# The `steps` stage of a hybrid layer taken into its samples' attention, and attention's rows stored tile by tile

## The reference

```
mod = silu(c) @ w_ada + b_ada            # 9 rows of c: the prompt's and 8 samples'
sh1, sc1, g1, sh2, sc2, g2 = split(mod, 6)
h = rmsnorm(x) * (1 + sc1) + sh1
z, xs, bm, cm, dtr, q, k, v, qi, ki, wi, gs, ga = split(h @ w_in)
# prompt: the indexer picks 256 keys per query, then softmax attention over them
# samples: the same over 256 cached keys in pages of 128 (a page table) and the new key
dt = softplus(dtr + dt_bias); A = -exp(a_log)
Acs = cumsum(dt * A) in chunks of 128    # decays of the chunked scan (32 heads)
xbc = silu(conv(xs, bm, cm))             # depthwise, causal, width 4
y_ssm = scan(xbc, dt, A) * silu(z), normed
x = x + g1 * ((sig(gs) * (y_ssm @ w1) + sig(ga) * (y_attn @ w2)) @ w_out)
h2 = rmsnorm(x) * (1 + sc2) + sh2
x = x + g2 * swiglu(h2)
```

## Time and profile before

| | |
|---|---|
| median of three runs | 2975.42 us |
| profiled execution, whole run | 2976.01 us |
| its span | 2974.3 us |
| busy in the span: PE, DVE, POOL, ACT | 2755.2, 1540.4, 810.6, 680.6 us |
| samples' attention | 942.8 to 1026.3 us of the span |
| `steps` | 1026.3 to 1087.2 us |
| start of `stream` | 1087.2 us |

### The profile page before, as it was taken

The page is one execution under the profiler, slowest core; times in us unless marked ns, Lnnn a source line. Parts: engine busy times, 40 slices in busy tenths (PEclk is TensorE's granted clock), DMA queues, the critical chain, the costliest instruction groups (busy, mean ns, idle before and its releaser), DMA issues. The chain is left out here.

```text
span 2974.3 us, 40645 instructions
## 1 busy us (share of the span) xinstructions
PE 2755.2 (93%) x16375; PEld 2343.0 (79%) x16375; DVE 1540.4 (52%) x2733; ACT 680.6 (23%) x1432; POOL 810.6 (27%) x486
## 2 busy tenths in 40 slices
PE   7999999998996678999979979998889999999997
PEld 4888556666785468999966669998878989898986
DVE  3313399905553357666459953554634242525155
ACT  3121211105774211221247731101210000000001
POOL 0000530004321124434326642231232222232220
PEclk9999999997998679999989989999989999999999
DMA  6110234520002144334156644333111111111111
GB/s 220 50 54 22 68 121 151 170 74 9 2 2 100 56 127 149 130 120 140 57 146 198 183 148 131 113 100 108 29 44 52 49 43 43 43 44 46 54 29 57
DMA packets 288663, 258.63 MB, mean 87 GB/s; under 512 B 21273, under 2 KB 265361, under 8 KB 288290
## 3 DMA queue, kind: packets, MB, share of 16 engines
q1 hardware_dynamic: 254780, 190.35, 21.3%
q10 hardware_dynamic: 26176, 56.16, 5.2%
q0 software_dynamic: 7520, 9.51, 1.0%
HBM read 191.04 MB, written 65.06 MB: 86 GB/s over the span
## 5 line engine op out<-in xcount | busy, mean ns | idle before, releaser
L2283 PE MATMUL ps<-h_lo,w_hi 128*128 128x344 f32 x1504 | 483.2, 321 | 18.0 <-DVE h_lo L2402 11.2
L2284 PE MATMUL ps<-h_hi,w_hi 128*128 128x344 f32 x1504 | 482.0, 321 | 0.0
L2285 PE MATMUL ps<-h_hi,w_lo 128*128 128x344 f32 x1504 | 481.9, 320 | 0.0
L2265 POOL CAST w_hi<-ring 128x2048 fp32r<-128x2048 f32 (+1 forms) x50 | 96.9, 1938 | 812.8 <-PE ps L2285 784.8
L2283 PEld LDWEIGHTS ps<-h_lo,w_hi 128*128 128x128 f32 x1504 | 284.5, 189 | 19.1 <-issue 18.4
L2285 PEld LDWEIGHTS ps<-h_hi,w_lo 128*128 128x128 f32 x1504 | 284.5, 189 | 0.0
L2284 PEld LDWEIGHTS ps<-h_hi,w_hi 128*128 128x128 f32 x1504 | 284.2, 189 | 0.2
L2283 PE MATMUL ps<-s_h_lo,s_w_hi 128*128 128x344 f32 x816 | 266.0, 326 | 0.0
L2284 PE MATMUL ps<-s_h_hi,s_w_hi 128*128 128x344 f32 x816 | 261.1, 320 | 0.0
L2285 PE MATMUL ps<-s_h_hi,s_w_lo 128*128 128x344 f32 x816 | 261.0, 320 | 0.0
L477 PE MATMUL ps<-ring,hT 128*128 128x256 f32 (+3 forms) x1152 | 237.5, 368 | 5.9 <-PEq L129 5.9
(11 more groups left out here) (416 smaller groups left out, 5213.2 us busy)
## 6 DMA issues: line engine op xcount, KB each, us to landing
ring<-in_w_ada SPq DMA_DIRECT2D x24, 1024.0 KB, 7.6
ring<-in_w_in SPq DMA_DIRECT2D x23, 1024.0 KB, 5.5
ring<-in_w_ffn_in SPq DMA_DIRECT2D x44, 512.0 KB, 4.8
ring<-in_w_in SPq DMA_DIRECT2D x24, 512.0 KB, 8.4
s_post<-post ACTq DMA_DIRECT2D x24, 512.0 KB, 2.6
post_chunk<-s_post SPq DMA_DIRECT2D x32, 384.0 KB, 3.6
ring<-in_w_ffn_out SPq DMA_DIRECT2D x10, 1024.0 KB, 5.0
s_sig<-sig ACTq DMA_DIRECT2D x16, 516.0 KB, 6.8
```

Of the source, the lines that this page charges most:

```text
L2265: self.nc.gpsimd.tensor_copy(hi, raw).then_inc(self.hi_done, 1)
L2283: nc.tensor.matmul(out, ah, bl, start=(i == 0), stop=False)
L2284: nc.tensor.matmul(out, ah, bh, start=False, stop=False)
L2285: mm = nc.tensor.matmul(out, al, bh, start=False, stop=(i == len(terms) - 1))
```

## The change

`steps` is no stage any more. Its parts stand in the lists of `attend_samples`, and the split of `hT` and of the first two slabs stands in `stream`:

- `attend` stores the rows of tiles 0 to 6 to `s_att` as they are scaled (SP). The last tile's rows are stored in `attend_samples`, behind the pages and the modulation rows.
- Index pages are issued 8 on SP and 8 on ACT, key pages 8 on POOL and 8 on SP. Values are fetched into the keys' buffer, two pages at a time, when TensorE has turned the keys of a sample.
- Of `s_mod` only the 4 times 9 rows that hold sums are fetched, with the bias in 9 more rows; the product with 45 rows of `pick` adds the bias as well. POOL's additions are gone. The gates are 9 rows each, and later stages spread the prompt's row while loading it.
- `k_head` is loaded over the modulation columns that were used, on ACT's queue.
- `s_h_lo` takes the place of `hT` itself. The first three units of `stream` are therefore plain fp32 products of the raw slab with `hT`, and DVE writes each third of `s_h_lo` after the unit that reads it.

```diff
 def attend(K, T):
         @block.sync
             sp.dma_start(own_head[:], A["k_head"][0:AH, 0:D]).then_inc(head_in, 16)
+            for s in K.finished:
+                sp.sem_clear(s)
+            for i in range(TT - 1):
+                cols = slice(P * i, P * i + P)
+                sp.wait_ge(y_scaled, 2 * i + 2)
+                sp.dma_start(A["s_att"]...[:, :, cols], T.qT[:, :, cols]).then_inc(rows_out, 16)
+            sp.wait_ge(rows_out, 16 * (TT - 1))
...
-def attend_samples(K, T):
+def attend_samples(K, T, S):
-        kpage, vpage = sb("kpage", [P, DEC, NPAGE, 256]), sb("vpage", [P, DEC, NPAGE, 256])
+        kpage = vpage = sb("kv_page", [P, DEC, NPAGE, 256])
...
         @block.gpsimd
-            load_pages(pool, "cache_k", kpage, k_in, 0, 16)
+            load_pages(pool, "cache_k", kpage, k_in, 0, 8)
         @block.sync
-            sp.dma_start(A["s_att"]...[:, :, 0:SEQ], T.qT[:, :, 0:SEQ]).then_inc(y_out, 16)
             sp.wait_ge(table_in, 16)
-            load_pages(sp, "cache_kidx", ipage, i_in, 0, 6)
-            load_pages(sp, "cache_v", vpage, v_in, 0, 16)
+            load_pages(sp, "cache_kidx", ipage, i_in, 0, 8)
+            load_pages(sp, "cache_k", kpage, k2_in, 8, 16)
+            for q in range(4):
+                sp.dma_start(mod[9 * q:9 * q + 9, :], A["s_mod"][32 * q:32 * q + 9, :]).then_inc(mod_in, 16)
+            sp.dma_start(mod[36:MR, :], A["b_ada"][0, 2 * D:6 * D].partition_broadcast(9)).then_inc(mod_in, 16)
+            sp.dma_start(A["s_att"]...[:, :, SEQ - P:SEQ], T.qT[:, :, SEQ - P:SEQ]).then_inc(y_out, 16)
+            for b in range(DEC):
+                sp.wait_ge(pe_key, b + 1)
+                load_pages(sp, "cache_v", vpage, v_in, NPAGE * b, NPAGE * b + NPAGE)
+            for i in range(2):
+                sp.wait_ge(gate_done, i + 1)
+                sp.dma_start(A["s_gates"][i], mod[0:9, 3 * D * i:3 * D * i + D]).then_inc(gate_out, 16)
             sp.wait_ge(y_done, 1)
...
 def stream(K, hT, S):
+    PLAIN = TC
             # sync, before slab RING is loaded
+                            if j == 0:
+                                sp.wait_ge(gemm, PLAIN)
         @block.gpsimd
             v.memset(pre[:, :, 0:CONV - 1], 0.0).then_inc(conv_zeroed, 1)
+            split_stream_slab(K, S, pool, 0)
...
             for j in range(NSLAB):
-                if 2 <= j + 1 < NSLAB:
+                if j + 1 < NSLAB:
         @block.tensor
+                if PLAIN <= u < 2 * PLAIN:
+                    pe.wait_ge(h_split, u - PLAIN + 1)
+                if u < PLAIN:
+                    for k in range(KB):
+                        a = mm(ps[:, u % 4, 0:CW], slab_of(K, first)[:, k, w], hT[:, k, cols], ...)
         @block.scalar
+            for c in range(TC):
+                a.copy(h_hi[:, :, cols], hT[:, :, cols]).then_inc(h_rounded, 1)
         @block.vector
+            for c in range(TC):
+                dve.wait_ge(h_rounded, c + 1)
+                dve.wait_ge(gemm, c + 1)
+                v.tensor_tensor(h_lo[:, :, cols], hT[:, :, cols], h_hi[:, :, cols]..., ALU.subtract)
             for f in range(FBS):
                 convolve(0, f)
```

More of the change, by code:

```diff
@@ L1035, in _ @@
             sp.wait_ge(y_out, 32)
+            sp.wait_ge(gate_out, 32)
         @block.tensor
@@ L1040, in _ @@
             i8, i4 = K.ident[0:DEC, 0:DEC], K.ident[0:DEC, 0:DEC]
-            pe.wait_ge(step, 1)
+            pe.wait_ge(step, 4)
             pe.wait_ge(who_in, 16)
@@ L1078, in _ @@
                 m.then_inc(pe_key, 1)
+            pe.wait_ge(dta_done, 1)
+            dta = S.dta[:].rearrange("p c h -> p (c h)")
+            mm(ps[:, 0, 0:NC], K.le[:], dta, start=True, stop=True)
+            mm(ps[:, 0, NC:2 * NC], K.gt[:], dta, start=True, stop=True)
+            mm(ps[:, 1, 0:NC], K.ones[:], dta, start=True, stop=True).then_inc(sums, 1)
+            pe.wait_ge(mod_in, 80)
+            pe.wait_ge(pick_done, 5)
+            for a, part in enumerate((1, 2)):
+                for k in range(KB):
+                    m = mm(ps[:, 2, (8 * a + k) * 9:(8 * a + k) * 9 + 9], mod[:, D * part + P * k:D * part + P * k + P], pick[:],
+                           start=True, stop=True)
+            m.then_inc(modT_ps, 1)
             pe.wait_ge(key_moved, DEC)
@@ L1087, in _ @@
             m.then_inc(pe_logit, 1)
+            pe.wait_ge(sdec, 1)
+            pe.wait_ge(modT_step, 1)
+            pe.wait_ge(head_in, 16)
+            for b in range(INNER // P):
+                m = mm(ps[:, 2, 144 + 17 * b:144 + 17 * b + 17], mod[0:HEADS, D + P * b:D + P * b + P], spread[:],
+                       start=True, stop=True)
+            m.then_inc(spread_ps, 1)
             pe.wait_ge(diag_done, 1)
@@ L1121, in _ @@
                                  accum_out=stat[:, 2:3]).then_inc(exp_done, 1)
+            for i, bank in enumerate((0, 4)):
+                act.wait_ge(gate_ps, i + 1)
+                nc.scalar.copy(mod[0:9, 3 * D * i:3 * D * i + D], ps[0:9, bank:bank + 2, :].rearrange("p a n -> p (a n)"))\
+                    .then_inc(gate_done, 1)
         @block.vector
@@ L1556, in unit @@
                 w, cols = slice(P * (i % 2), P * (i % 2) + P), slice(CW * c, CW * c + CW)
+                if u < PLAIN:
+                    for k in range(KB):
+                        a = mm(ps[:, u % 4, 0:CW], slab_of(K, first)[:, k, w], hT[:, k, cols], start=(k == 0), stop=(k == KB - 1))
+                    a.then_inc(gemm, 1)
+                    return
                 product(nc, ps[:, u % 4, 0:CW], [
@@ L2464, in _ @@
                 r = P if b == 0 else DEC
-                sp.dma_start(gate[0:r, b, :], A["s_gates"][b, 0:r, :]).then_inc(gate_in, 16)
+                sp.dma_start(gate[0:r, b, :], A["s_gates"][0, 0].partition_broadcast(P) if b == 0 else A["s_gates"][0, 1:9, :]).then_inc(gate_in, 16)
             for t in range(9):
@@ L2790, in program @@
         mid = ctx.enter_context(ExitStack())
+        with ExitStack() as place:
+            h_lo = place.enter_context(nc.sbuf_tensor("s_h_lo", [P, KB, NT], F32R, side="right"))
         K.hT = hT = mid.enter_context(nc.sbuf_tensor("hT", [P, KB, NT], F32, side="right"))
```

317 lines of the change are left out of this document (122 added, 195 removed).

## The result

The changed kernel takes 2924.56 us (median of 4 runs, 2923.5 to 2928.67), the kernel before beside it 2974.73 (2972.35 to 2977.69): ratio 0.9832, 95% interval 0.982 to 0.9843. The forecast was 2934, so the direction was right and the gain, 50 us, is 9 us larger than the 41 worked out. The time lies within the range (2921 to 2948), but not in the forecast's own band (2930 to 2941): it falls into that of the hidden lag or the faster clock (2918 to 2930). The profiled execution takes 2925.0 us with a span of 2923.3, 51.0 us less than before.

The account below looks back on a forecast made before the run. `steps` was taken as a chain of waits, bound by no engine. From 2976.0 us, -60.9 + 9.6 + 2.6 + 7.5 = -41.2 gave 2934.8, less 0.6 to the median: 2934 us, range 2921 to 2948.

Parts of the forecast that it names:

- hidden lag: Rival in the head of `stream`: DVE's lag costs TensorE nothing, 2927 us; chance 0.25 shared with a faster clock.
- faster clock: Rival: clock also rises in the denser samples' attention, 2919 us with DVE's lag hidden; shared chance 0.25.
- Steps gone, -60.9: Stage `steps`, between samples' attention and `stream`, goes with its block, saving 60.9 us.
- Samples' attention, +9.6: Samples' attention takes over products and gates from `steps`, gains from earlier pages, and ends 9.6 us later.
- Rows, no gain: Modulation and gate products in samples' attention: 45 rows in place of 128 given no gain.
- Cover: Samples' attention: softplus, modulation rows, value pages, head table and tile stores, plus semaphore clears in `stream`, cost nothing.
- Plain units, +2.6: Head of `stream`: three plain fp32 units at 4.64 us instead of 3.77 for split ones, plus 2.6 us.
- VectorE's lag, +7.5: Head of `stream`: subtractions and three colliding POOL splits delay DVE, so TensorE waits 7.5 us, once.
- Late pages: Rival: pages in samples' attention only 1.7 us earlier and one more DVE collision, 2943 us; chance 0.17.
- work only moved: Rival: late modulation rows or value pages make the joined block as long as both were, 2975 us; chance 0.02.
- VectorE as the bound of all of `stream`: Rival: DVE never catches up, each slab's split hits a convolution TensorE waits for, 83 us, 3017 us; chance 0.04.

Follow-up runs that it names:

- run with all rows: Changed kernel, but all 128 rows of the modulation sums fetched and sent through TensorE instead of 45; ratio 0.9837 to the kernel before.
- the run without them: Changed kernel, but attention's rows stored as one 4 MB store ahead of the index pages instead of tile by tile; ratio 0.986 to the kernel before.
- a relieved GpSimd: Changed kernel, but ScalarE instead of GpSimd fills the segment weights, behind its casts; ratio 0.9831 to the kernel before.
- later waits: Changed kernel, but ScalarE's and TensorE's waits for VectorE in the head of `stream` placed behind later units; 2926.39 us, ratio 0.9828 to the kernel before.
- three tries: Changed kernel with slab 1 split directly behind slab 0, segment-weight fill on ScalarE, or first convolution before the subtractions; ratios 0.9836, 0.9831, 0.9827 to the kernel before.
- slab 1 first: Changed kernel, but GpSimd splits weight slab 1 directly behind slab 0, ahead of the segment-weight fill and decays' store; ratio 0.9836 to the kernel before.
- the last experiments: Changed kernel with waits for VectorE placed later, then also GpSimd's second diagonal before a split, then also gates earlier; ratios 0.9828, 0.9825, 0.9816 to the kernel before.

## Why the prediction was right, and where it was short

**Steps gone, -60.9.** Right: no stage stands between the samples' attention and `stream`.

**Samples' attention, +9.6.** This term was mis-sized; the block took 84.5 us where 93.1 were worked out. The step that failed is the last sentence of the term, that TensorE's rows are kept as they were. Counted from the block's start, by the rows above against the earlier trace rows: the sums and modulation products took 5.1 us, not 9.0 (-4.0); mask product and logits 9.5, not 11.0 (-1.5); the spread product 3.7, not 7.0 (-3.3); transposes to output products -0.7; the gates 7.0, not 5.8 (+1.2). The pages were 2.7 us earlier than I took (12.5 us into the block), but the scores and key turns behind them ran at a lower clock than in the kernel before, so that only 0.3 of it is left (-0.3). Together -8.6. The windows of the scores and key turns, of the changed kernel and of the one before (PEclk is the third number from the end):

```profile
954.70:980.90 26.20, 25.37 (x81) 9.77 (x82) 9.29 (x36) 9.19 (x19) 0.00 (x0) 0.51 0.47 107
```

```profile
963.10:986.70 23.60, 22.51 (x80) 8.68 (x80) 5.87 (x20) 9.32 (x19) 2.68 (x5) 0.63 0.34 101
```

So the larger part of the 8.6 us is the granted clock, but not nearly all. Where it was higher (modulation, mask, logits, spread, transposes) some 8.8 us were won, where it was lower (scores and key turns, gates) 3.6 lost, 5.2 net. The pages' 2.7 us and some 0.6 us by which the three sums took less than the 2.0 worked out are the rest. That the clock's gains and losses leave no more than this is luck. The 8 us that the prediction named as a possible gain were meant for the mask product and the logits, which gave 1.5: the clock rose mostly at other products. The run with all rows shows that the modulation products don't owe their time to their size. What set the level of the clock at each product stays open: it fell behind or within the modulation products with a gap and without one. The Trainium skill, TensorE: Matmul & The Clock Gate, Part 1: The HAM clock gate, puts it so that the default state is throttled and activity releases it. The trace agrees in part: the full clock came at the end of the unbroken key turns, at 980.2. The fall to 0.50 inside the unbroken middle, and the output products, at 0.50 while the window 1000.5 to 1026.8 shows TensorE busy 22.2 of 26.3 us, are not explained by it alone.

**Rows, no gain.** Right: with all 128 rows the block was no longer (83.7 us).

**Cover.** Right: neither the modulation rows nor the value pages were waited for, and the stores by tile cost attention nothing (the block starts at 942.3, as in the run without them, and before at 942.8).

**Plain units, +2.6.** Three took from 1030.32 to 1044.58, 4.75 each: +2.9.

**VectorE's lag, +7.5.** The mechanism was right: waits for ScalarE, the tail copies and the diagonal, 6.1 us, once, within 72 us of the start. The third subtraction ended 21.3 us in (21.9 worked out); three splits cost VectorE 4.4, 5.9 and 5.9 us; the diagonal's product came at 71.1, not 72.8. With the plain units the head gave back 8.5 us, not 10.1, 1.6 less; with the block's 8.6 that makes 10.2, and the span came out 9.8 below the sum. One reading of the earlier trace rows says too much: VectorE's next step was begun beside GpSimd's 4.92 us, at 1117.38, and held for 5.51 us where its neighbours took 1.29, until 1.1 us after GpSimd's end. It is exclusion all the same. What the prediction didn't see is that the lag is a length of VectorE's chain, not a wait at one place: order, a relieved GpSimd and later waits all left VectorE's squares at 115.7 to 119.8 us, and only taking the splits out of `stream` brought 106.1.

**Rivals.** Hidden lag: no, but its second number, for a faster clock, named the larger part of what the forecast missed. Late pages, work only moved, VectorE as the bound of all of `stream`: none showed.

## What to carry to other kernels

When short products get another place in TensorE's list, price them at both levels of the clock: here the same product cost 3.74 or 6.98 us. Closing the waits around them doesn't settle which: the clock fell and rose inside an unbroken stretch. When VectorE is late in a chain, look for the next place where TensorE needs it before moving a wait: of 6.1 us of waits aimed at 2.0 were won there, of 13.4 us 4.8. And order alone didn't undo the collisions of VectorE and GpSimd in three tries; it chose which instruction was hit.

## What the hardware showed beside that

A very small VectorE instruction can cost as much as a long one beside GpSimd: the copy of 128x11 took 4.57 us and a product of 128x48 took 4.53 us while GpSimd subtracted 128x2048, against 0.16 and 0.21 alone. It goes both ways: GpSimd's cast of 128x2048 took 1.89 us alone and 3.91 beside VectorE's subtraction. The Trainium skill, SBUF — State Buffer, Who interferes with whom, lists copies among what can take the shared ports, and these rows agree.

The granted clock differs between runs of the same kernel also where TensorE is busy, and the time with it: the changed kernel took 2931.4 us at a mean of 0.959 and 2923.9 at 0.962. A stretch of `stream`, 150 us behind the edit, shows the same, first in the changed kernel (both of its profiles have 0.97), then with slab 1 first:

```profile
1200.00:1300.00 100.00, 98.36 (x601) 97.11 (x600) 64.55 (x57) 18.50 (x34) 36.01 (x14) 0.97 0.39 122
```

```profile
1200.00:1300.00 100.00, 99.19 (x627) 97.95 (x625) 68.44 (x62) 18.99 (x35) 36.13 (x14) 1.00 0.41 130
```

The two executions took the same time in all (2925.0 and 2924.8 us). The changed kernel's own runs lie 7.5 us apart with no edit, more than the last experiments were after, so distances inside a stage had to be read instead.
